# A longer lead and more buffers in the attention loop of a two-layer decoder trunk, with value products taken two pairs at a time

## What is computed

```python
score = jnp.where(pos[None, None, :] <= tb[None, :, None], score, -jnp.inf)
_, idx = lax.top_k(score, n_sel)                 # 128 keys of each query
logits = jnp.einsum('bqhd,bqkhd->bhqk', qb, kg) * (HEAD_DIM ** -0.5)
p = jax.nn.softmax(logits, axis=-1)
y_attn = jnp.einsum('bhqk,bqkhd->bqhd', p, vg)   # 8 heads of 64, 512 tokens
...
y_mem = memory_attention(mq, mem_n, w_kv, ...)   # 4 heads, 256 memory tokens
x = x + jnp.concatenate([y_attn, y_pool, y_mem], axis=-1) @ w_out[l]
```

## Time and profile before

| | |
|---|---|
| median of 3 runs | 1859.08 us (1858.18 to 1864.09) |
| profiled execution, its own time | 1859.6 us |
| span of the profiled execution | 1857.8 us, so 1.8 us lie around it |
| TensorE busy | 1845.5 us (99% of the span) |
| DVE, ACT, POOL busy | 1185.5, 993.7, 667.5 us |
| granted TensorE clock, mean | 1.000 |
| attention loop, layer 1 / layer 2 | 480.35 to 546.50 / 1402.00 to 1468.13 us |

### The profile page before, as it was taken

One profiled execution on the slowest core, in us unless ns is written; L12 is line 12 of the kernel. 1 busy time (PEld: TensorE's weight loads), 2 busy tenths in 40 slices (PEclk: granted clock), 3 DMA queues, 4 the chain that ended last, 5 costly groups with the idle time before them and its releaser, 6 DMA issues. The chain is left out here.

```text
span 1857.8 us, 33596 instructions
## 1 busy us (share of the span) xinstructions
PE 1845.5 (99%) x11685; PEld 1624.9 (87%) x11685; DVE 1185.5 (64%) x1925; ACT 993.7 (53%) x1610; POOL 667.5 (36%) x530
## 2 busy tenths in 40 slices
PE   9999999999999999999999999999999999999999
PEld 7999988887778899998889999888877789999887
DVE  6989821378754998941098998114787459999311
ACT  6444554575656544454474445546657564444642
POOL 2366611112511266631115666111216012666210
DMA  8433398888238633378874334988881485333885
GB/s 230 122 103 100 114 218 190 183 203 199 63 92 192 139 111 102 101 190 195 192 171 114 97 106 124 218 191 202 188 202 34 100 205 128 110 95 112 203 196 133
DMA packets 78087, 277.23 MB, mean 149 GB/s; under 512 B 8624, under 2 KB 10928, under 8 KB 77744
## 3 DMA queue, kind: packets, MB, share of 16 engines
q1 hardware_dynamic: 48960, 175.67, 30.4%
q0 software_dynamic: 28464, 98.05, 29.7%
q10 hardware_dynamic: 576, 2.36, 0.4%
HBM read 175.91 MB, written 2.10 MB: 96 GB/s over the span
## 5 line engine op out<-in xcount | busy, mean ns | idle before, releaser
L560 POOL DMA_DIRECT2D w_lo<-raw x179 | 153.9, 869 | 769.9 <-ACT w_lo L1258 730.8
L632 POOL TENSOR_TENSOR w_lo<-s_sum,w_hi 128x512 fp32r<-128x512 f32 x200 | 318.0, 1604 | 244.0 <-ACT w_hi L1306 244.0
L1257 ACT ACTIVATE w_hi<-raw 128x1024 fp32r<-128x1024 f32 x155 | 164.0, 1058 | 338.3 <-PE bank L688 322.9
L688 PE MATMUL bank<-t_hi,w_hi 128*128 128x256 f32 x1152 | 326.7, 284 | 2.1 <-DVE zf L1787 2.1
L688 PE MATMUL bank<-t_lo,w_hi 128*128 128x256 f32 x1152 | 326.0, 283 | 0.0
L688 PE MATMUL bank<-t_hi,w_lo 128*128 128x256 f32 x1152 | 325.9, 283 | 0.0
L688 PE MATMUL bank<-a_hi,w_hi 128*128 (+1 forms) x832 | 324.6, 390 | 0.0
L688 PE MATMUL bank<-a_lo,w_hi 128*128 (+1 forms) x832 | 323.8, 389 | 0.0
L1306 ACT ACTIVATE w_hi<-s_sum 128x512 fp32r<-128x512 f32 x216 | 127.7, 621 | 275.3 <-DVE s_sum L1769 269.4
L688 PE MATMUL bank<-a_lo,w_lo 128*128 (+1 forms) x704 | 273.9, 389 | 0.0
L1699 DVE TENSOR_TENSOR a_hi<-zf,a_lo (+1 forms) x88 | 64.0, 731 | 322.3 <-ACT a_lo L1366 322.2
(11 more groups left out here) (210 smaller groups left out, 3884.7 us busy)
## 6 DMA issues: line engine op xcount, KB each, us to landing
raw<-weights SPq DMA_DIRECT2D x326, 512.0 KB, 4.2
w_lo<-raw POOLq DMA_DIRECT2D x179, 512.0 KB, 6.2
x<-x_t SPq DMA_DIRECT2D x4, 512.0 KB, 7.1
t_lo<-t_sum POOLq DMA_DIRECT2D x4, 512.0 KB, 6.6
b_lo<-hn POOLq DMA_DIRECT2D x4, 512.0 KB, 7.3
mem<-mem_t ACTq DMA_DIRECT2D x2, 1024.0 KB, 7.1
out_t<-x SPq DMA_DIRECT2D x8, 256.0 KB, 2.1
const<-consts SPq DMA_DIRECT2D x1, 481.5 KB, 9.8
```

Of the source, the lines that this page charges most:

```text
L560: G.dma_start(w_lo[:, s], raw[:, s], accum_op=ALU.add).then_inc(w_ready[pos], 16)
L632: G.tensor_tensor(out=fast_weight(l, e, product, 0, True), in0=s_sum[i - 1][:, :], in1=fast_weight(l, e, product, 0, False).bitcast(f32), ...
L688: return nc.tensor.matmul(out_, lhsT, rhs, start=start, stop=stop, skip_group_check=True)
L1257: nc.scalar.activation(w_hi[:, s], raw[:, s], ACT.Copy).then_inc(w_hi_done, 1)
```

## The change

LAG goes from 4 to 6. Transposed probabilities get 8 buffers (`PT`), probabilities 8 (`AHEAD`), masked logits 4. TensorE takes value products only in every second step, n = 10, 14, ..., 54, and then those of two pairs. DVE rounds out 0 and out 1 in the loop, at units 9 and 11; out 2 and out 3 are rounded by ACT behind its loop, ahead of out 4.

```diff
-LAG = 4
-OUT_ROUND_UNITS = (9, 11, 21, 23)
+LAG = 6
+PT = 8
+AHEAD = 8
+OUT_ROUND_UNITS = (9, 11)
...
-    pt = [place(f"pt{i}", T, h_at + i * tile_b) for i in range(4)]
+    pt = [place(f"pt{i}", T, h_at + (i % 4 + 2 * (i - i % 4)) * tile_b) for i in range(PT)]
...
-           [place(f"prob{i}", T, h_at + (4 + i) * tile_b)[:, :] for i in range(2)]
+           [place(f"prob{i}", T, h_at + (4 + i) * tile_b)[:, :] for i in range(2)] + \
+           [place(f"prob{i}", T, h_at + (10 + i) * tile_b)[:, :] for i in range(2, AHEAD - 2)]
+    logit = [t2[:, 0:T], t2[:, T:2 * T]] + \
+            [place(f"logit{i}", T, a_hi_at + (8 + i) * tile_b)[:, :] for i in range(2)]
...
-        if n >= 4:
-            eng.wait_ge(pv_done[n % 2], l * (UNITS // 2) + (n // 2 - 1))
-        copy(pt[n % 4][:, 0:blocks * P], bank[2 + n % 2][:, 0:blocks * P])\
+        if n >= PT:
+            eng.wait_ge(pv_done[n % 2], l * (UNITS // 2) + ((n - PT) // 2 + 1))
+        copy(pt[n % PT][:, 0:blocks * P], bank[2 + n % 2][:, 0:blocks * P])\
...
-                    if 0 <= n - LAG - 2 < UNITS:
+                    if n % 4 == 2 and n >= LAG + 4:
+                        times_v(n - LAG - 4)
                         times_v(n - LAG - 2)
...
-                    if n >= 4:
-                        act.wait_ge(ptp_done, l * UNITS + (n - 3))
-                    nc.scalar.activation(prob[n % 4][:, 0:blocks * P], chunk(t2, n % 2, T, blocks * P),
+                    if n >= AHEAD:
+                        act.wait_ge(ptp_done, l * UNITS + (n - AHEAD + 1))
+                    nc.scalar.activation(prob[n % AHEAD][:, 0:blocks * P], logit[n % 4][:, 0:blocks * P],
...
-                for k in range(DC - 1):
+                for k in range(len(OUT_ROUND_UNITS) - RING, DC - 1):
                     round_ahead(l, MIX_BASE["out"] + k)
...
-                    if n >= 2:
-                        dve.wait_ge(p_ready, l * UNITS + (n - 1))
+                    if n >= 4:
+                        dve.wait_ge(p_ready, l * UNITS + (n - 3))
```

More of the change, by code:

```diff
@@ L1141, in transpose_p @@
                         last = nc.tensor.transpose(bank[2 + n % 2][:, b * P:(b + 1) * P],
-                                                   prob[n % 4][:, b * P:(b + 1) * P], con(C_ID, P))
+                                                   prob[n % AHEAD][:, b * P:(b + 1) * P], con(C_ID, P))
                     last.then_inc(ptp_done, 1)
@@ L1165, in times_v @@
                             last = mm(y_bank(g)[half * HD:(half + 1) * HD, j * P:(j + 1) * P], val,
-                                      pt[(n + half) % 4][:, b * P:(b + 1) * P], b == 0, b == blocks - 1)
+                                      pt[(n + half) % PT][:, b * P:(b + 1) * P], b == 0, b == blocks - 1)
                             if b == blocks - 1:
@@ L2097, in mask_and_max @@
                         bias = score[:, score_at[i]:score_at[i] + blocks * P]
-                    if n >= 2:
-                        dve.wait_ge(p_ready, l * UNITS + (n - 1))
+                    if n >= 4:
+                        dve.wait_ge(p_ready, l * UNITS + (n - 3))
                     wait_apart(dve, logit_done[n % 2], l * (UNITS // 2) + (n // 2 + 1))
-                    V.tensor_tensor_reduce(out=chunk(t2, n % 2, T, blocks * P),
+                    V.tensor_tensor_reduce(out=logit[n % 4][:, 0:blocks * P],
                                            in0=logit_bank[n % 3][:, 0:blocks * P], in1=bias,
```

## The result

The changed kernel took 1881.8 us (median of 4 runs, 1880.21 to 1883.22) against 1859.65 us before: ratio 1.0118, 95% interval 1.0106 to 1.0131, **22 us slower**. The direction was forecast; the size was not: 1872.0 was predicted, with a range up to 1880.

What follows compares the result with a forecast made beforehand. TensorE, busy for 1845.5 of 1857.8 us, was the bound. Loop +2.0 and out 2 +4.2 made 6.2 us a layer, 12.4 for both, on 1859.6: 1872.0 us, range 1865 to 1880.

Steps and rivals of the forecast that it cites:

- the wait for out 2: Behind the loop, TensorE waits for out 2, ready after 8.4 us but wanted after 4.2: 4.2 us a layer.
- short steps: Loop steps without value products, which no longer hide DVE's copy behind its masks: new waits of +2.2 us a layer.
- the sum: Loop terms of one layer: -1.8 switches, -1.7 old waits, +2.2 short steps, +3.1 split, +0.2 loop's end: +2.0 us.
- the term of the split: In the loop, DVE's half of `split_y` moves into short steps, between two masks: +3.1 us a layer.
- the cost of a lead of six: At the loop's end, the last pair's value products directly follow their own transposes' step: +0.2 us a layer.
- the last two: Splits of the last two groups in a layer, standing behind the loop's masks: claimed to cost nothing.
- rival A: Clock falls in the wait for out 2, a dozen matmuls slower: 2.6 us a layer, 1877.2 us; chance 0.26.
- B: Buffers let DVE and ACT run ahead, loop wins 3.5 us a layer, out 2 still waits: 1861.0 us; chance 0.10.
- C: B's loop gain, and out 2 in time behind the loop: -3.5 us a layer, 1852.6 us; chance 0.04.
- the wait for DVE's copy: In the loop, old waits of 1.7 us a layer expected gone; new ones in short steps, not loosened by buffers.
- its switches: In the loop, value-product runs fall from 24 to 12 a layer, each saving 0.15 us: -1.8 us.

Runs made afterwards that it cites:

- e2: The kernel before with only out 2 and out 3 rounded by ACT behind the loop, nothing else of the change: 1872.4 us.
- e10: The changed kernel with DVE's split two units later, out 2 and out 3 still rounded behind the loop: 1873.8 us.
- e1: The changed kernel with all four output slots rounded in the loop again (units 9, 11, 21, 23): 1869.2 us.
- e7: e1 with the lead back at four units, value products still of two pairs in every second step: 1864.6 us.
- e11: The kernel before with DVE's split two units later and nothing else: 1859.3 us, ratio 0.9993.
- e5: e1 with DVE's split of a group's result two units later (group end + LAG + 4): 1860.7 us.
- e3: e1 with the value products of one pair in every step, lead of six and buffers kept: 1863.9 us.
- e4: The changed kernel with 16 filler matmuls (128x512, result thrown away) ahead of the wait for out 2: 1875.9 us.
- e9: e5 with out 0 to 3 rounded in the loop at units 9, 11, 45 and 48: 1860.7 us, ratio 1.0001.
- e8: The kernel before with out 2 and out 3 rounded at units 45 and 48 instead of 21 and 23: 1859.8 us, ratio 1.0000.
- e6: e1 with three filler matmuls (128x384) ahead of the transposes of each of steps 40, 42 and 44: 1867.4 us.

## Why the prediction was right or wrong

**Right: the wait for out 2.** 4.2 us were predicted and 3.9 measured, in every kernel with that edit (e2, e10, the change); idle time, releaser and each link of the chain stand where the text put them. e2 shows it by itself.

**Half right: that the short steps lose their cover and that the split costs there.** The loop at full clock (e1) costs 3.6 and 3.2 us more than before, where the sum had +2.0. e7 puts 2.0 on pairs with a lead of four, splits in the short steps included. Moving the split gives back 2.8 us, near the 3.1 that it was priced at, and in the kernel before (e11) only 0.3. After that e5 keeps 2.2 us of waits in the first loop, the size of the term for the short steps, but they are for ACT's copies (1.1) and DVE's masks (1.1), not for DVE's copy (0.4) as the prediction had it.

**Wrong in its working: the term of the split.** It counted DVE's own time, and only in short steps. DVE also stands still for ACT's half: 2.3 us a layer before (the earlier trace rows shows it), 2.8 in the change. And e3 has the same waits of DVE and TensorE without short steps, so their place in short steps isn't all of it; the lead of six, with ACT's `copy_rt` now ahead of its half, has a part. The price of an instruction that was moved is its duration and the wait in front of it.

**Wrong: the cost of a lead of six.** It was set at 0.2 us, the end of the loop. e3 has 1.8 us at full clock with single products, and e1 is 1.6 and 1.1 above e7. Only 0.41 us of e3's waits for DVE's copy lie at the loop's end, and they too stand behind a split, one of the last two that were taken to cost nothing; most of the others stand behind splits as well. e5, with the same lead and the split moved, is only 0.8 and 0.4 above before, which suggests that the greater part goes with the split's place. No run has the lead of six with single products and the split later, so the exact division stays open.

**The step that failed: the sum has no term for the clock; it was kept at 1.00.** The clock was rival A, with 0.26, and there with one fall a layer. That fall came behind the wait for out 2 in both layers of every profiled execution that has this wait without a filler (the change, e2, e10), at 1.5 to 1.8 us (3.0 in e10) instead of the 2.6 priced; in the change half clock began 0.8 and 1.6 us after the restart and lasted some 3.4 us. The rule named there from the Trainium skill's "TensorE: Matmul & The Clock Gate" (section "Why this matters for your kernels"), that idle gaps of a few us bring half rate, was right for this wait; e4 agrees, with no half clock once 3.8 us of filler take the gap away. What neither that rule nor the rival had: a second fall in each loop, with no gap above 0.8 us, worth 1.9 and 3.6 us. Why it comes stays open: it came in three of the four loops of the change and e4, and not in e1, whose waits are nearly the same (2.5 us for DVE's copy in the first loop against 2.2).

The profiled execution took 10.5 us more than the forecast. Half clock is 9.1 of them (1.8 and 1.8 behind the wait, 1.9 and 3.6 in the loops), the loops at full clock 2.8; the wait for out 2 was 0.6 shorter than priced, and the rest of the kernel 0.8.

**Rivals B and C** fell. B wanted the loop 3.5 us shorter by the buffers alone; they don't touch the wait for DVE's copy, and even with both repairs (e9) the loop is 0.1 and 0.3 us longer than before. C wanted out 2 in time, and it came 3.9 us later than before.

**Why the gain does not show.** The pairing seems to save its switches: TensorE's busy time in the loop is 65.10 us before and 63.99 in e5, 1.1 less, where 1.8 were forecast. But its idle time there rises from 1.05 to 2.96 us (2.21 in e9), so that the waits take as much back.

## What to carry to other kernels

Uneven steps on the bounding engine need cover for the short ones, not on average: look at which buffer is reused one step later (here two PSUM banks), since more buffers elsewhere don't loosen it, and at which instructions of the other engines land in the short steps, or ahead of one another, when a lead changes, with the waits in front of them. Work that is put "behind the loop" starts after the loop's last dependent instruction, so add the whole chain to the landing of its DMA and set it against what the bounding engine has left. Price a wait of TensorE of two us and more with its clock, and keep it busy with a filler if the wait can't be avoided.

## What was not expected of the hardware

- The clock fell in the loop with TensorE idle for no more than 0.76 us at a time; it was busy for 3.63 of the 5 us before. In e1 no fall followed the same 5 us with the same waits. The kernel before, at 9.8 of 10 us busy in the same place, kept 1.00.
- The fall in the loop comes and goes under the same instructions: in both loops of the change and the first of e4 (71.6, 73.0 and 71.6 us), not in the second of e4 (69.4 us).
- Outside the loop, half clock followed every idle time of 2.1 us or more in the traces (2.12 and 3.15 us in e7, 2.33 in e8, 2.45 in e6, 2.79 in e9, 3.7 to 3.8 in the change, e2 and e10). Behind those of 1.1 to 1.6 us, the kernel's first matmuls left aside, the granted clock stayed at 1.00.
- After the same idle time of 3.7 to 3.8 us the 36 matmuls behind it took 9.7 to 9.9 us in the change and e2 and 11.2 in e10, against 8.2.
